# Mixer attention ordered by query block, with the last block's selection rounds between its units, and score matmuls of two heads issued in turn

## The chip, the cores and the metric

The kernel runs on one core of a Trainium2 chip. The metric is device time in microseconds (us) of one execution, the median of the runs shown. Profiled executions are single ones; their own time stands beside their span.

## The reference

A sequence of 512 tokens of width 1024 goes through two blocks, all in float32. The first block has a pooling layer and an attention layer with 16 heads of 64 in three groups of dilations 1, 4 and 16, each followed by a gated feed-forward layer. The second block has two layers, each with a feed-forward layer, a mixer and another feed-forward layer. The mixer is what the change is mostly about. In short:

```
p = h @ w_in                       # u, va, q, k, v, iq, ik, iw
a_out = gelu(u) * (tril(w_s) @ gelu(va) + b_s)            # gating, chunks of 128
score[t, s] = sum_h iw[t, h] * relu(iq[t, h] . ik[s])     # 4 index heads, s <= t
keep = the 128 largest of score[t, :]
b_out = softmax(q k^T / 8 over keep) v                    # 8 heads of 64
y = concat(a_out, b_out) @ w_out
```

## The kernel before, in words

Every float32 product is made of three matmuls on a high and a low part: high x high, high x low, low x high (`mm3`, L1701). Weights arrive in slabs of 128 x 1024; ScalarE rounds a slab to its high part (`split_hi`, L604), VectorE (`split_lo`, L1024) or, for slabs 10 to 22 of a mixer projection, GpSimd (`project_lo`, L564) subtracts to get the low part. Two split slabs exist at a time. Engines are ordered by hand: each has its own program, and semaphores count steps.

**Projection (`project`, L1859 on TensorE, L1276 on VectorE, L738 on ScalarE).** 23 slabs, of which the last two are left to the mixer. In slots 6 to 8 TensorE makes the index scores of query blocks 1 to 3 (`index_scores`, L1889): for each block four heads, head by head, each with its three matmuls; heads alternate between partitions 0 to 63 and 64 to 127, since one head has 64 of the 128 rows. ScalarE takes the relu, VectorE adds them up with their weights into `score`. Then 16 selection rounds follow (`topk_round`, L1397; `ROUNDS`, L1341, says how many after which slab). A round finds the eight largest of each row (MAX8, L1400) and overwrites them (MATCH_REPLACE8, L1406), for blocks 1, 2 and 3 of 256, 384 and 512 columns. At the end the overwritten places become the mask (L1393). Block 0 keeps everything causal.

**Mixer (`mix`, L1950 on TensorE, L816 on ScalarE, L1427 on VectorE).** 32 units u, a head and a query block each; head u // 4 and block u % 4, so that the width n goes 128, 256, 384, 512 over and over. For a unit, TensorE makes the scores (L1956) in one of three PSUM banks, three units ahead; VectorE adds the mask and takes the row minimum of the negated scores (`mask_scores`, L1432); ScalarE takes the exponential and its sum (L841); TensorE transposes the n / 128 blocks (L2035); ScalarE writes their high part (`probs_hi`, L822), VectorE the low part (`probs_lo`, L1442). After the four units of a head TensorE multiplies with the values (`values`, L1965), 12 matmuls over 512, 384, 256 and 128 columns, and ScalarE copies the output (`o_out`, L831). TensorE fills its time: in units 0 to 7 the rest of the projection (`last_u`, L1988), in units 16 to 31 the gated half of the output projection (`first_part`, L2002), six matmuls of 512 columns a unit (`FILL`, L449). In units 9 to 12 the gating matmuls stand (`sgu`, L1978), VectorE follows with two operations (`sgu`, L1411) and a low part (`sgu_lo`, L1423). ScalarE's gelus of two tiles (L853) stand in unit 8, with a change of its table to gelu and back. At the end the reciprocal sums are transposed (L2048), split and spread over the heads' rows (L2057, L2058), multiplied in (L1494), and the rest of the output projection (`out_rest`, L2060) begins.

**First attention (`dilated_attention`, L2079).** 22 steps: the six heads of dilation 1 have two steps of two blocks, the other ten heads one step of four blocks of 128. Score banks are three (`SCORE_BANKS`, L404), and scores run three steps ahead, one step after each step's transposes. After the last step of a head its values follow.

## Time and profile before

| | us |
|---|---|
| runs (three) | 3250.24, 3252.34, 3247.52; median 3250.24 |
| profiled execution, its own time | 3245.89 |
| its span | 3244.2 |
| mean granted clock of TensorE | 0.973 of full |
| TensorE busy | 3110.7 |
| VectorE busy | 1751.6 |
| ScalarE busy | 1193.7 |
| first attention, first to last transposes | 668.4 to 729.0 |
| first mixer, first fill to the rest of the output projection | 1701.4 to 1806.3 |
| second mixer, first fill to the last transposes | 2733.2 to 2828.8 |

A busy share is the time in which an engine executes something; matmuls are pipelined, so a busy TensorE can still be at a fraction of its rate, and the start times of neighbouring matmuls tell more than their durations. A wait is put down to the instruction that released it last. The stretches used below: 1653.9 to 1700.0 is the end of the first mixer's projection; 1701.4 to 1723.3 has units 0 to 7 (from the first fill to the transposes of unit 8); 1723.3 to 1750.6 units 8 to 15; 1750.6 to 1797.0 the rest up to the transposes of unit 31; 1797.0 to 1806.3 the tail. 668.4 to 700.1 has the twelve steps of dilation 1 in the first attention, 700.1 to 729.0 the other ten.

### The profile page before, as it was taken

What the parts mean: (1) busy time and instruction counts of PE and PEld (TensorE: products, weight loads), DVE (VectorE), ACT (ScalarE), POOL (GpSimd) and SP (SyncE); (2) the same over time, 40 slices, a digit from 0 to 9 for tenths busy, and PEclk for the clock granted to TensorE, in tenths of its full rate; (3) what the DMA queues carried; (4) which work ended last, traced back from release to release, by engine and by line L of the source; (5) the groups of instructions that cost most, each with busy time, mean ns of one, the idle gap of its engine ahead of it and who ended that gap; (6) DMA issues with size and microseconds to landing.
All of it is one profiled execution on the core that took longest, in us unless ns stands there. A gap on an engine that the chain in (4) does not pass through costs nothing.

```text
span 3244.2 us, 38749 instructions
## 1 busy us (share of the span) xinstructions
PE 3110.7 (96%) x14007; PEld 2546.1 (78%) x14007; DVE 1751.6 (54%) x2784; ACT 1193.7 (37%) x1687; POOL 124.9 (4%) x117
## 2 busy tenths in 40 slices
PE   7899999999999999999999999999999998899998
PEld 5788888877888878888776788887888876678887
DVE  5577535655785366634684666324332576553323
ACT  3332323463233244432334443324442334444422
POOL 0000000000000000000030000000000012000000
PEclk8999999988999999999899999999999999899999
DMA  3355333203554335533220355322333322023332
GB/s 116 122 183 186 106 97 95 89 20 96 183 187 136 97 117 187 174 95 98 70 83 22 115 189 187 98 94 85 96 97 97 96 72 65 27 82 95 96 103 78
DMA packets 262904, 351.28 MB, mean 108 GB/s; under 512 B 16664, under 2 KB 208536, under 8 KB 262808
## 3 DMA queue, kind: packets, MB, share of 16 engines
q1 hardware_dynamic: 240768, 270.57, 26.9%
q0 software_dynamic: 21360, 79.01, 7.5%
q8 instruction: 60, 0.98, 0.1%
q10 hardware_dynamic: 680, 0.43, 0.0%
q14 instruction: 36, 0.29, 0.0%
HBM read 348.75 MB, written 2.10 MB: 108 GB/s over the span
## 4 chain that ended last, share of the span: by engine, by line
PE 84%; DVE 9%; ACT 4%; issue 2%; DMA 0%; POOL 0%; SPq 0%; DVEq 0%; ACTq 0%
PE bank L1703 28%; PE bank L1704 27%; PE bank L1705 27%; ACT w_hi L613 1%; DVE a_score L1406 1%; DVE a_m L1400 1%; DVE w_lo L1028 1%; DVE rot L1309 1%; DVE sumsq L1041 1%; PE bank L2035 1%; DVE work L1081 1%; DVE turned L1308 0%; DVE h_lo L1087 0%; PE bank L1744 0%; ACT probs L900 0%
## 5 line engine op out<-in xcount | busy, mean ns | idle before, releaser
L1028 DVE TENSOR_TENSOR w_lo<-raw,w_hi 128x1024 fp32r<-128x1024 f32 x482 | 589.7, 1224 | 1195.4 <-ACT w_hi L613 1194.8
L1703 PE MATMUL bank<-h_hi,w_hi 128*128 128x512 f32 x2864 | 1137.8, 397 | 28.3 <-POOL w_lo L571 11.7
L1705 PE MATMUL bank<-h_hi,w_lo 128*128 128x512 f32 x2864 | 1125.1, 393 | 0.0
L1704 PE MATMUL bank<-h_lo,w_hi 128*128 128x512 f32 x2864 | 1124.1, 393 | 0.0
L613 ACT ACTIVATE w_hi<-raw 128x1024 fp32r<-128x1024 f32 x508 | 537.6, 1059 | 1364.4 <-PE bank L1705 1359.9
L1703 PEld LDWEIGHTS bank<-h_hi,w_hi 128*128 128x128 f32 x2864 | 543.6, 190 | 158.1 <-issue 41.1
L1705 PEld LDWEIGHTS bank<-h_hi,w_lo 128*128 128x128 f32 x2864 | 543.1, 190 | 115.6
L1704 PEld LDWEIGHTS bank<-h_lo,w_hi 128*128 128x128 f32 x2864 | 544.2, 190 | 109.8
L1703 PE MATMUL bank<-act_hi,w_hi 128*128 (+1 forms) x1120 | 435.9, 389 | 1.0 <-DVE w_lo L1028 1.0
L1705 PE MATMUL bank<-act_hi,w_lo 128*128 (+1 forms) x1120 | 435.7, 389 | 0.0
L1704 PE MATMUL bank<-act_lo,w_hi 128*128 (+1 forms) x1120 | 435.7, 389 | 0.0
L1703 PEld LDWEIGHTS bank<-act_hi,w_hi 128*128 128x128 f32 x1120 | 210.3, 188 | 45.2 <-issue 1.4
L1705 PEld LDWEIGHTS bank<-act_hi,w_lo 128*128 128x128 f32 x1120 | 210.3, 188 | 43.5
L1704 PEld LDWEIGHTS bank<-act_lo,w_hi 128*128 128x128 f32 x1120 | 210.3, 188 | 43.5
L1109 DVE SCALAR_TENSOR_TENSOR ada_acc<-ada_w,cact,ada_acc 128x512 f32<-128x512 f32 x252 | 189.2, 751 | 7.7
L698 ACT ACTIVATE act_hi<-work 128x512 f32 (+1 forms) x132 | 82.1, 633 | 161.2 <-DVE work L1148 89.5
L533 POOL DMA_DIRECT2D ada_w<-in_ada_w_dram x72 | 54.3, 755 | 1414.4 <-DVE ada_acc L1109 988.5
L1151 DVE TENSOR_TENSOR act_lo<-work,act_hi 128x512 f32 (+1 forms) x132 | 87.0, 692 | 20.6 <-ACT act_hi L698 20.4
L1438 DVE CUSTOM_DVE_ANT_0 bank<-bank,a_masks 128x128 f32<-128x128 f32 (+1 forms) x64 | 31.9, 499 | 94.8 <-PE bank L1705 94.7
L571 POOL TENSOR_TENSOR w_lo<-raw,w_hi 128x1024 fp32r<-128x1024 f32 x26 | 61.8, 2387 | 254.4 <-ACT w_hi L613 254.4
L613 ACT ACT_TABLE_LOAD x45 | 57.7, 1283 | 7.8 <-issue 7.0
L630 ACT ACTIVATE sq<-xT 128x512 f32<-128x512 f32 x70 | 43.8, 627 | 36.3 <-DVE xT L1092 33.1
(288 smaller groups left out, 2368.3 us busy)
## 6 DMA issues: line engine op xcount, KB each, us to landing
raw<-in_ffn_w_in_dram SPq DMA_DIRECT2D x176, 512.0 KB, 3.5
ada_w<-in_ada_w_dram POOLq DMA_DIRECT2D x72, 1024.0 KB, 5.6
raw<-in_ffn_w_out_dram SPq DMA_DIRECT2D x88, 512.0 KB, 3.7
raw<-in_ffn_w_gate_dram SPq DMA_DIRECT2D x44, 512.0 KB, 3.8
raw<-in_ffn_w_up_dram SPq DMA_DIRECT2D x44, 512.0 KB, 3.8
raw<-in_ffn_w_down_dram SPq DMA_DIRECT2D x44, 512.0 KB, 3.7
raw<-in_mix_w_in_dram SPq DMA_DIRECT2D x44, 512.0 KB, 3.6
raw<-in_attn_w_qkv_dram SPq DMA_DIRECT2D x24, 512.0 KB, 3.6
```

The costliest lines, as they stand in the source:

```text
L533: pool.dma_start(ada_w[:, half], w[:, 4 * half:4 * half + 4, bass.ds(i * 512 + (f % 2) * N_MOD * 512, 512)])\
L571: nc.gpsimd.tensor_tensor(w_lo[:, n % SPL, :], raw[:, n % RAW, :], w_hi[:, n % SPL, :].bitcast(F32), ALU.subtract).then_inc(s_lo, 1)
L613: nc.scalar.activation(w_hi[:, nb % SPL, :], raw[:, nb % RAW, :], ACT.Copy).then_inc(s_hi, 1)
L630: nc.scalar.activation(part, xT[:, k, :], ACT.Square, scale=size).then_inc(s_sq, 1)
L698: nc.scalar.activation(act_hi[:, bass.ds(i * 2 + c, 1), :], work[:, 2 + c:3 + c, :], ACT.Copy).then_inc(s_ahi, 1)
L1028: V.tensor_tensor(w_lo[:, nb % SPL, :], raw[:, nb % RAW, :], w_hi[:, nb % SPL, :].bitcast(F32), ALU.subtract).then_inc(s_lo, 1)
L1041: V.tensor_tensor(total, total, part, ALU.add).then_inc(s_sum, 1)
L1109: ins = V.scalar_tensor_tensor(out=ada_acc[:], in0=w, scalar=cact[:, k:k + 1], in1=ada_acc[:], op0=ALU.mult, op1=ALU.add)
L1151: V.tensor_tensor(act_lo[:, bass.ds(i * 2 + c, 1), :], work[:, 2 + c:3 + c, :], act_hi[:, bass.ds(i * 2 + c, 1), :].bitcast(F32), ALU.subt ...
L1703: T.matmul(dst, wh, mh, start=first, stop=False)
L1704: T.matmul(dst, wh, ml, start=False, stop=False)
L1705: return T.matmul(dst, wl, mh, start=False, stop=last)
```

## The change

- **Order of units.** Unit u is head u % 8 of query block u // 8, so the widths are 128 for units 0 to 7, 256 for 8 to 15, 384, then 512. Probabilities have a ring of three, and values are made per unit (two units behind its transposes) in matmuls of 128 columns, 3 (b + 1) of them for block b. `o_out` copies four heads of a block by two instructions. 240 value matmuls take the place of 96.
- **Selection.** `topk_round` in the projection has blocks 1 and 2 only. VectorE makes the 16 rounds of block 3 in units 0 to 15 of the mixer, one in each: MAX8 ahead of the mask of unit u + 2, MATCH_REPLACE8 behind it and ahead of the low part of unit u. The mask of block 3 is made at unit 16.
- **Scores of two heads in turn.** The scores of a pair of heads (rows 0 to 63 and 64 to 127, two PSUM banks) are issued as one group, the same term of either head in turn, at every second unit and two units ahead; so too the index scores (which now wait for both relus before), and in the first attention, where the steps of dilation 1 are reordered to (h, 0), (h + 1, 0), (h, 3), (h + 1, 3), four banks are used and a pair of steps is issued at every odd step.
- **Moved.** Output fills stand in units 14 to 29, gating matmuls in 8 to 11, VectorE's gating in 8 to 11 with low parts in 10 to 13, additions to x from unit 16, slab splits of the output projection from 18 and 19 on. The first scores wait for the gelus of two tiles. The reciprocal sums come at unit 31 ahead of its low part; their transposes and ScalarE's copy of them come ahead of the last values and output copies. GpSimd's two waits for all values count units instead of heads.

The diff, cut to its core (indentation shortened):

```diff
-SCORE_BANKS = (0, 1, 6)
+STEP_BANKS = (0, 1, 6, 7)
...
-for h in range(HEAD_GROUPS[0][1]):
-    A0.append((h, 0, [(4 * h, 0, 0, 0, P, 0), (4 * h + 1, P, 0, P, 2 * P, P)]))
-    A0.append((h, 3, [(4 * h + 2, 2 * P, P, 0, 2 * P, P), (4 * h + 3, 3 * P, 2 * P, 2 * P, 2 * P, P)]))
+for pair_at in range(0, HEAD_GROUPS[0][1], 2):
+    for h in (pair_at, pair_at + 1):
+        A0.append((h, 0, [(4 * h, 0, 0, 0, P, 0), (4 * h + 1, P, 0, P, 2 * P, P)]))
+    for h in (pair_at, pair_at + 1):
+        A0.append((h, 3, [(4 * h + 2, 2 * P, P, 0, 2 * P, P), (4 * h + 3, 3 * P, 2 * P, 2 * P, 2 * P, P)]))
...
-FILL = {u: ("u", 2 * u) for u in range(8)} | {u: ("out", 2 * (u - 16)) for u in range(16, 32)}
+FILL = {u: ("u", 2 * u) for u in range(8)} | {u: ("out", 2 * (u - 14)) for u in range(14, 30)}
...
-            h, b = u // 4, u % 4
+            n = (u // 8 + 1) * P
             act.wait_ge(s_tr, u0 + u + 1)
-            if b == 0 and h >= 2:
-                act.wait_ge(s_pv, h0 + h - 1)
-            dst = b_["PTh"][:, h % 2, :].rearrange("p (n q) -> p n q", q=P)[:, b:b + 3 * b + 1:3, :]
-            nc.scalar.activation(dst, bank[2 + u % 2][:, 0:(b + 1) * P].rearrange("p (n q) -> p n q", q=P), ACT.Copy)\
-                .then_inc(s_pth, 1)
-        def o_out(h):
-            act.wait_ge(s_pv, h0 + h + 1)
-            rows = slice(HD * (h % 2), HD * (h % 2) + HD)
-            nc.scalar.activation(b_["oT"][rows, h // 2, :], bank[4][0:HD, :], ACT.Copy).then_inc(s_o, 1)
+            if u >= 3:
+                act.wait_ge(s_pv, t["p0"] + u - 2)
+            nc.scalar.activation(b_["PTh"][:, u % 3, 0:n], bank[2 + u % 2][:, 0:n], ACT.Copy).then_inc(s_pth, 1)
+        def o_out(g):
+            b, j = g // 2, 2 * (g % 2)
+            act.wait_ge(s_pv, t["p0"] + 4 * g + 4)
+            for x in range(2):
+                ins = nc.scalar.activation(b_["oT"][HD * x:HD * x + HD, j:j + 2, b * P:(b + 1) * P],
+                                           bank[4][0:HD, 2 * x * P:2 * x * P + 2 * P].rearrange("p (n q) -> p n q", q=P),
+                                           ACT.Copy)
+            ins.then_inc(s_o, 1)
...
-                        topk_round(bufs, (1, 2, 3))
+                        topk_round(bufs, (1, 2))
...
-        for u in range(3):
+        for u in range(2):
             mask_scores(u)
         for u in range(nu):
-            if u + 3 < nu:
-                mask_scores(u + 3)
+            if u < 16:
+                dve.wait_ge(s_dve, steps[0])
+                largest()
+            if u == 16:
+                dve.wait_ge(s_dve, steps[0])
+                keep_taken(bufs, 3)
+            if u + 2 < nu:
+                mask_scores(u + 2)
+            if u < 16:
+                take_largest()
+            if u == nu - 1:
+                dve.wait_ge(s_exp, u0 + nu)
+                V.reciprocal(bufs["fine"][:, 5, :, 0:nh], bufs["den"][:, 0:nu].rearrange("p (b h) -> p b h", b=NB))\
+                    .then_inc(s_on, 1)
...
+            y, b, j = 12 * (m - 1) + x0, x0 // 4 + 1, x0 % 4 // 2
+            if x0 == 0:
+                pe.wait_ge(s_post, PO0[m] + 3)
+                pe.wait_ge(s_wi, m)
+            else:
+                pe.wait_ge(s_relu, y)
+            q, k = slice(b * P, (b + 1) * P), slice(0, (b + 1) * P)
+            for n, (a, c) in enumerate((("iqTh", "ikTh"), ("iqTh", "ikTl"), ("iqTl", "ikTh"))):
+                for x in (0, 1):
+                    r = slice(HD * x, HD * x + HD)
+                    ins = T.matmul(bank[6 + x][:, k], bufs[a][r, j, q], bufs[c][r, 0, k], start=n == 0, stop=n == 2)
+                    if n == 2:
+                        ins.then_inc(s_idxmm, 1)
...
+            b, j = u // 8, u % 8 // 2
+            if u >= 2:
+                pe.wait_ge(s_exp, u0 + u - 1)
             q, k = slice(b * P, (b + 1) * P), slice(0, (b + 1) * P)
-            mm3(bank[MIX_BANKS[u % 3]][:, k], bufs["qTh"][r, h // 2, q], bufs["qTl"][r, h // 2, q],
-                bufs["kTh"][r, h // 2, k], bufs["kTl"][r, h // 2, k], True, True).then_inc(s_scmm, 1)
-        def values(h):
-            c = h // 2
-            pe.wait_ge(s_pt, u0 + 4 * h + 4)
-            if h:
-                pe.wait_ge(s_o, t["h0"] + h)
-            for k in range(NB):
-                v = slice(c * P + HD * (h % 2), c * P + HD * (h % 2) + HD)
-                pt = slice(4 * k * P, 4 * k * P + (NB - k) * P)
-                ins = mm3(bank[4][0:HD, k * P:S], bufs["vNh"][:, k, v], bufs["vNl"][:, k, v],
-                          bufs["PTh"][:, h % 2, pt], bufs[f"PTl{h % 2}"][:, pt], k == 0, k == NB - 1)
+            for n, (a, c) in enumerate((("qTh", "kTh"), ("qTh", "kTl"), ("qTl", "kTh"))):
+                for x in range(2):
+                    r = slice(HD * x, HD * x + HD)
+                    ins = T.matmul(bank[MIX_BANKS[(u + x) % 3]][:, k], bufs[a][r, j, q], bufs[c][r, j, k],
+                                   start=n == 0, stop=n == 2)
+                    if n == 2:
+                        ins.then_inc(s_scmm, 1)
+        def values(u):
+            b, h = u // 8, u % 8
+            pe.wait_ge(s_pt, u0 + u + 1)
+            if u % 4 == 0 and u:
+                pe.wait_ge(s_o, t["h0"] + u // 4)
+            at = (h % 4 // 2 + 2 * (h % 2)) * P
+            for k in range(b + 1):
+                v = slice(h * HD, h * HD + HD)
+                pt = slice(k * P, (k + 1) * P)
+                ins = mm3(bank[4][0:HD, at:at + P], bufs["vNh"][:, k, v], bufs["vNl"][:, k, v],
+                          bufs["PTh"][:, u % 3, pt], bufs["PTl"][:, u % 3, pt], k == 0, k == b)
...
+        pe.wait_ge(s_actT, AT0[f"out{m}"] - 2)
         scores(0)
-        pe.wait_ge(s_actT, AT0[f"out{m}"] - 2)
-        scores(1)
-        scores(2)
         for u in range(nu):
             if u in FILL:
                 what, step = FILL[u]
             pe.wait_ge(s_exp, u0 + u + 1)
             if u >= 2:
                 pe.wait_ge(s_pt, u0 + u - 1)
-            for k in range(u % 4 + 1):
+            for k in range(u // 8 + 1):
                 ins = T.transpose(bank[2 + u % 2][:, k * P:(k + 1) * P], bufs["P"][:, u % 2, k * P:(k + 1) * P], ident)
             ins.then_inc(s_tr, 1)
-            if u + 3 < nu:
-                scores(u + 3)
-            if 9 <= u < 13:
-                sgu(u - 9)
-            if u % 4 == 1 and u >= 5:
-                values(u // 4 - 1)
-        values(nh - 1)
-        pe.wait_ge(s_hlo, H0[f"attn{m}"] + 4)
+            if u % 2 == 0 and u + 2 < nu:
+                scores(u + 2)
+            if 8 <= u < 12:
+                sgu(u - 8)
+            if u >= 2:
+                values(u - 2)
+        values(nu - 2)
         pe.wait_ge(s_on, OT0[m] + 1)
         for b in range(NB):
             ins = T.transpose(bank[6][0:nh, b * P:(b + 1) * P], bufs["fine"][:, 5, b, 0:nh], ident)
         ins.then_inc(s_otr, 1)
+        values(nu - 1)
...
-            if s >= 3:
+            if s >= 4:
                 pe.wait_ge(s_exp, s - 2)
-            h = A0[s][0]
-            r = slice(HD * (h % 2), HD * (h % 2) + HD)
-            for _, q, k, off, n, _ in A0[s][2]:
-                ins = mm3(bank[SCORE_BANKS[s % 3]][:, off:off + n], bufs["qTh"][r, h // 2, q:q + P],
-                          bufs["qTl"][r, h // 2, q:q + P], bufs["kTh"][r, h // 2, k:k + n], bufs["kTl"][r, h // 2, k:k + n],
-                          True, True)
-            ins.then_inc(s_scmm, 1)
+            j, blocks = A0[s][0] // 2, A0[s][2]
+            for i, (_, q, k, off, n, _) in enumerate(blocks):
+                for t, (a, c) in enumerate((("qTh", "kTh"), ("qTh", "kTl"), ("qTl", "kTh"))):
+                    for x in (0, 1):
+                        r = slice(HD * x, HD * x + HD)
+                        ins = T.matmul(bank[STEP_BANKS[(s + x) % 4]][:, off:off + n], bufs[a][r, j, q:q + P],
+                                       bufs[c][r, j, k:k + n], start=t == 0, stop=t == 2)
+                        if i == len(blocks) - 1 and t == 2:
+                            ins.then_inc(s_scmm, 1)
...
-        for s in range(3):
-            scores(s)
+        scores(0)
+        scores(2)
         for s in range(n_steps):
             pe.wait_ge(s_exp, s + 1)
             if s >= 2:
             for k in range(width(A0[s]) // P):
                 ins = T.transpose(bank[2 + s % 2][:, k * P:(k + 1) * P], bufs["P"][:, s % 2, k * P:(k + 1) * P], ident)
             ins.then_inc(s_tr, 1)
-            if s + 3 < n_steps:
+            if s % 2 and s + 3 < n_steps:
```

## Rows read from the trace of the kernel before

**Rows 1.** The page: span, and busy time of each engine.

```profile
span 3244.2 us, 38749 instructions
...
PE 3110.7 (96%) x14007; PEld 2546.1 (78%) x14007; DVE 1751.6 (54%) x2784; ACT 1193.7 (37%) x1687; POOL 124.9 (4%) x117
```

**Rows 2.** By stretch: length; PE, PEld, DVE, ACT, POOL busy; granted clock; DMA share; GB/s.

```profile
1653.90:1700.00 46.10, 38.46 (x171) 31.07 (x171) 37.66 (x108) 15.19 (x23) 17.29 (x8) 0.96 0.27 80
1701.40:1723.30 21.90, 21.90 (x105) 15.86 (x105) 7.89 (x26) 9.95 (x30) 0.00 (x0) 1.00 0.16 49
1723.30:1750.60 27.30, 20.24 (x95) 14.83 (x95) 15.12 (x33) 14.17 (x32) 0.00 (x0) 0.75 0.06 20
1750.60:1797.00 46.40, 46.07 (x228) 33.68 (x229) 23.21 (x59) 20.75 (x56) 0.00 (x0) 1.00 0.11 33
1797.00:1806.30 9.30, 5.89 (x30) 3.44 (x27) 5.11 (x9) 3.00 (x5) 1.55 (x2) 0.93 0.36 119
668.40:700.10 31.70, 31.28 (x194) 26.70 (x194) 17.75 (x72) 21.24 (x73) 0.00 (x0) 0.79 0.00 1
700.10:729.00 28.90, 25.45 (x231) 22.57 (x231) 17.09 (x78) 26.16 (x93) 0.00 (x0) 0.94 0.01 1
```

**Rows 3.** Waits, 1560 to 1700 us (first mixer projection): total, times, longest.

```profile
ACT L812 <- DVE a_vNl L1290: 9.7, 1, 9.7
...
PE bank L1703 <- POOL w_lo L571: 5.9, 3, 2.8
```

**Rows 4.** Order of time (start, us): matmuls on PE behind the third stall.

```profile
1685.82 0.63 PE L1703 MATMUL bank<-h_hi,w_hi 128*128 128x512 f32 x1
1686.24 0.63 PE L1704 MATMUL bank<-h_lo,w_hi 128*128 128x512 f32 x1
```

**Rows 5.** VectorE by form, 1600 to 1807 us: busy, mean ns, idle before.

```profile
L1406 DVE MATCH_REPLACE8 a_score<-a_m,a_score 128x512 f32<-128x512 f32 x16 | 10.8, 676 | 0.0
L1400 DVE MAX8 a_m<-a_score 128x8 f32<-128x512 f32 x16 | 10.8, 676 | 0.0
...
L1028 DVE TENSOR_TENSOR w_lo<-raw,w_hi 128x1024 fp32r<-128x1024 f32 x7 | 8.5, 1217 | 2.2 <-ACT w_hi L613 2.2
...
L1406 DVE MATCH_VALUE_LOAD a_score<-a_m,a_score 128x8 f32 x48 | 3.8, 78 | 0.0
L1438 DVE CUSTOM_DVE_ANT_0 bank<-bank,a_masks 128x256 f32<-128x256 f32 x8 | 3.5, 433 | 16.3 <-PE bank L1705 16.3
...
L1425 DVE TENSOR_TENSOR h_lo<-work,h_hi 128x512 fp32r<-128x512 f32 x4 | 2.7, 681 | 0.0
...
L1447 DVE TENSOR_TENSOR a_probsT_lo<-bank,probsT_hi 128x256 fp32r<-128x256 f32 x4 | 1.7, 422 | 1.9 <-ACT probsT_hi L828 1.9
```

**Rows 6.** Order of time: index scores of two heads, opposite row halves.

```profile
1602.82 0.40 PE L1704 MATMUL bank<-a_ikTl,a_iqTh 64*128 64x512 f32 x2
1603.05 0.40 PE L1705 MATMUL bank<-a_ikTh,a_iqTl 64*128 64x512 f32 x2
```

**Rows 7.** Order of time: mixer scores of one head, then a fill.

```profile
1713.52 0.39 PE L1704 MATMUL bank<-a_kTl,a_qTh 64*128 64x512 f32 x1
...
1713.75 0.39 PE L1705 MATMUL bank<-a_kTh,a_qTl 64*128 64x512 f32 x1
...
1714.07 0.50 PE L1703 MATMUL bank<-h_hi,w_hi 128*128 128x512 f32 x1
```

**Rows 8.** Order of time: first and last of 12 value matmuls, 128 columns.

```profile
716.01 0.27 PE L1703 MATMUL bank<-a_probsT_hi,h_hi 128*64 128x128 f32 x1
...
716.71 0.22 PE L1705 MATMUL bank<-a_probsT_hi,h_lo 128*64 128x128 f32 x1
```

**Rows 9.** Order of time: the gelu pause of the mixer.

```profile
1728.71 0.29 DVE L1447 TENSOR_TENSOR probsT_lo<-bank,probsT_hi 128x128 fp32r<-128x128 f32 x1 [3.40 <-ACT probsT_hi L828]
```

**Rows 10.** Order of time: last transposes, start of the coefficient spreading.

```profile
1796.86 0.60 PE L2035 MATMUL bank<-squares,probs 128*128 128x128 f32 x4
...
1802.87 0.47 PE L2057 MATMUL bank<-a_cTh,sel 8*128 8x512 f32 x1 [1.61 <-issue]
```

99 lines of the change are left out of this document (43 added, 56 removed).

## The prediction

> **What bounds the kernel now.** The page comes first: TensorE is busy 96% of the span, VectorE 54%, ScalarE 37% [rows 1]. A share over the whole span says little on three stages that the change touches, so I cut them into stretches next [rows 2]. In the mixer of the first mixer layer, units 0 to 7 take 21.9 us and TensorE is busy all of it at full clock: TensorE is the bound. Units 8 to 15 take 27.3 us, TensorE busy 20.2 of them at a granted clock of 0.75 (between the levels of 1.2 and 2.4 GHz): here a chain over ScalarE and VectorE sets the pace. Units 16 to 31 take 46.4 us with TensorE busy 46.1: TensorE again. The tail to the rest of the output projection is 9.3 us with 5.9 busy. The second mixer layer has the same stretches to 0.1 us, so every term below counts twice. The first attention has a half where TensorE is busy 31.3 of 31.7 us at clock 0.79, and a half where ScalarE is busy 26.2 of 28.9 us.
>
> The waits of the projection show what the page hides: TensorE waits 5.9 us in three stalls for slabs split by GpSimd, and ScalarE, which feeds GpSimd, sits 9.7 us behind a value tile of VectorE [rows 3]. VectorE is busy 37.7 us of that 46.1 us stretch [rows 2], with selection rounds. So VectorE, not the weights, ends those stalls. Behind the third stall matmuls start 0.42 us apart [rows 4] where 0.23 us is usual [rows 7]; the stretch's clock of 0.96 means 8% of 46.1 us at the lower level, half of which is lost, 1.8 us.
>
> **Projection.** Sixteen rounds on the last block leave it, each a MAX8 and a MATCH_REPLACE8 on 512 columns with a value load: 0.676 + 0.676 + 0.078 = 1.43 us [rows 5], together 22.9 us of VectorE. That is four times the stalls. What is late next is the ordinary slab chain, which keeps up where VectorE isn't in it. Ceiling 5.9 + 1.8 = 7.7 us, floor 3 (one stall, the longest being 2.8, goes); I take 6.5, near the ceiling, since the relief is so much larger than the stall.
>
> **Index scores.** The program issues three matmuls of one head, then three of the next in the other row half, but they start in twos, 0.23 us per two [rows 6]. They run side by side already, so interleaving them by hand costs and brings nothing; the wait for both older relus may add some 0.5 us, inside the bounds. The Trainium skill (TensorE: Matmul & The Clock Gate, Part 3) says that matmuls are strictly ordered by program in start and end. By that rule the two heads could not have overlapped before and the twelve head-blocks (about 6 us a layer at 384 columns each) would now halve, the total falling 6 us more; the measurement decides against it.
>
> **Mixer, units 0 to 7.** A unit is now a head of query block 0. Its TensorE work falls: score pairs side by side, half as many changes between full-row and half-row matmuls; 48 fill matmuls at 0.23 us stay (11.0), the rest falls from 10.9 to about 5. But VectorE gets a round per unit: 1.43 + mask 0.43 + low part 0.42 = 2.28 [rows 5] (the forms of 256 columns, a bound from above for 128), eight times 18.2, and one slab split of 1.2. TensorE 16, VectorE at most 19.4: I take 18.5, so -3.4; between -4.5 and 0. The round sits in VectorE's order ahead of the low part of the same unit, for which the transposes of the unit after next wait; up to there TensorE may run ahead.
>
> **Units 8 to 15.** The gelu pause of ScalarE stays: its first low part comes at 1728.71, 5.4 us into the stretch [rows 2, 9]. From there VectorE has, for units 8 to 13, five rounds with mask (1.86 each, 9.3), six low parts (2.5), four gating pairs and four of their low parts (12 x 0.68 = 8.2), a slab split (1.2): 21.2 us. Then a new wait: the output fills start at unit 14 instead of 16, and the first needs the last gating low part of unit 13. TensorE then owes three fills (18 x 0.23 = 4.1), transposes (four, 0.11 each [rows 10]), a score pair (0.7) and twelve value matmuls at 0.064 (0.70 / 11) [rows 8]: 6.0 us before the transposes of unit 16. Sum 5.4 + 21.2 + 6.0 = 32.6 against 27.3: +5.3. Bounds: 0 if instructions overlap as they do in rounds of three blocks and the fills slip under VectorE, +10 if TensorE is at the lower clock there. I take the sum.
>
> **Units 16 to 31.** Now: 96 fill matmuls at 0.23 (22.1), scores 15360 columns at 0.45 ns, from 0.23 us for 512 (6.9), 40 transposes (4.4), values 15360 columns (6.9): 40.3. The other 6.1 us are 32 changes of row mode, 0.19 each; 0.09 of one is seen directly, 0.32 instead of 0.23 [rows 7]. Afterwards: 13 fills remain behind the first transposes (78 x 0.23 = 17.9); 19200 score columns in twos (4.3); 52 transposes (5.7); 144 value matmuls at 0.064 (9.2); 14 changes (2.7). That is 39.8, and about 1.2 at the end, where units 30 and 31 have no fill to cover their exponentials: 41.0, -5.4. VectorE is busy 23.2 us of this stretch now [rows 2] and gets one mask of 0.4 us more, so TensorE's work hides it; without that cover the mask and low part of a unit would stand on the path. Bounds -7 and -1 (the latter without overlap of pairs).
>
> **Tail.** The last values shrink from 3840 columns (1.7) to 12 short matmuls (0.8), and the coefficients are turned and split ahead of them, which takes the 1.6 us of issue wait [rows 10] and their own transposes; two output copies come behind the values instead of one. -2.7, between -3.5 and -1.
>
> **First attention.** The first half loses half of 16128 score columns (7.3 us, more at clock 0.79) and half its mode changes, but ScalarE's 21.2 us and its chain are near: -3. The second half has ScalarE at 26.2 of 28.9 us: -1. Bounds -8 (ScalarE's own time) and +2 (longer stretches at the lower clock, since two steps' scores now stand ahead of each values).
>
> **Sum.** Mixer -3.4 + 5.3 - 5.4 - 2.7 = -6.2; with -6.5 a layer gives -12.7; twice -25.4; first attention -4: -29.4 us. The profiled execution took 3245.9 us (span 3244.2 and 1.7 around it), so 3216.5; it lies 4.3 below the median of the three runs, so 3221 for a median.
>
> **Rivals.** (A) The sum above, 3212 to 3233. (B) VectorE's rounds are absorbed: units 8 to 15 keep 27.3 us and the first attention gains two more: 3221 - 10.6 - 2 = 3208. For it: back-to-back VectorE records overlap. Against: gating and rounds fall together. (C) The change doesn't do what it says: float pairs of 64 rows in the mixer don't run side by side. Third stretch +4.3, first +1, twice, and 4 in the first attention: 3236. The index pairs speak against it [rows 6]. (D) Slower: the rounds bound units 0 to 15. There VectorE's 7.9 + 15.1 busy us [rows 2] and 22.9 make 45.9 of a present 49.2, and each low part waits behind a match. The forecast exposes 1.9 us of the 22.9 a layer; gains elsewhere are 6.5 + 5.4 + 2.7 + 2 = 16.6. Above that the kernel is slower; wholly exposed, (22.9 - 16.6) x 2 = +12.6: 3263. Against it: TensorE's queue runs ahead by up to two units. (E) The clock: should the thinner TensorE work of units 8 to 15 and short matmuls keep it at 1.2 GHz for 23 of the 41 us of the third stretch, 11.5 us a layer go back, 3244, and no change can be told. Against it: that stretch ran at 1.00 behind one at 0.75.
>
> **Chances.** A 0.60, B 0.16, C 0.12, E 0.05, D 0.07. A measurement here tells about 0.2%, 6.5 us, from no change; A, B and C are faster by more, E the same, D slower. Range 3205 to 3241: A whole, most of B, and C.
>
> **What would show it.** Projection: no wait of ScalarE for a value tile of 9 us, TensorE's wait for GpSimd near 0. Units 0 to 7 about 18.5 us, VectorE over 90% busy; 8 to 15 about 33 us with a wait ahead of the fill of unit 14; from the transposes of unit 16 to those of 31 about 41 us, TensorE without waits; mixer scores of two heads starting in twos 0.23 us apart at 512 columns. The forecast is wrong if the 5.9 us stay, or if VectorE ends TensorE's waits throughout.

## The result, and the profile after

The changed kernel takes 3209.9 us (median of four runs, 3209.0 to 3216.6) against 3248.9 for the kernel before (four runs, 3246.9 to 3252.3): a ratio of 0.988, 95% interval 0.986 to 0.990. It is faster by 39 us. The forecast was 3221 us in a range of 3205 to 3241, so the direction and the range were right, and the size was 10 us short: 3209.9 lies below the 3212 to 3233 us that the prediction gave its own sum (rival A), and 2 us from the 3208 of rival B.

The profiled execution took 3216.56 us, 29.3 less than the profiled one of before (3245.89). That is the -29.4 of the sum almost to the digit, and largely by accident, as the next table shows: this execution lies 6.6 us above the median of its own kernel. A second profile of the same kernel was therefore taken beside the experiments (`after_again`, own time 3208.30). The table has starts of transposes, read from the order of time of each trace; differences between neighbouring rows give the stretches.

| us from the start | before | after | after_again |
|---|---|---|---|
| first attention, first transposes | 668.39 | 669.16 | 666.75 |
| first attention, last transposes | 728.74 | 727.40 | 720.65 |
| first mixer, unit 0 | 1702.90 | 1693.97 | 1687.53 |
| unit 8 | 1723.30 | 1709.81 | 1703.33 |
| unit 16 | 1753.68 | 1744.20 | 1737.72 |
| unit 31 | 1796.86 | 1784.70 | 1778.17 |
| second mixer, unit 0 | 2733.79 | 2710.84 | 2704.25 |
| unit 8 | 2754.25 | 2726.81 | 2718.80 |
| unit 16 | 2784.55 | 2759.80 | 2752.47 |
| unit 31 | 2827.68 | 2800.30 | 2792.98 |
| own time | 3245.89 | 3216.56 | 3208.30 |

From before to after_again, in that order: first attention 60.4 to 53.9 (-6.4); from there to unit 0, which holds the first projection, -7.3; units 0 to 7 20.4 to 15.8 (-4.6) and in the second layer 20.5 to 14.6 (-5.9); units 8 to 15 30.4 to 34.4 (+4.0) and 30.3 to 33.7 (+3.4); units 16 to 31 43.2 to 40.5 (-2.7) and -2.6; from unit 31 to the unit 0 of the second layer (tail, feed-forward layers, second projection) 936.9 to 926.1 (-10.8); the rest -2.9, and the part before the first attention -1.6. The two profiles of the changed kernel differ mostly in the first attention (58.2 against 53.9).

The page of the changed kernel, answering [rows 1]. TensorE has 29 us less to do, VectorE as much as before: the change took nothing from it, it only moved it.

```profile
span 3214.9 us, 39389 instructions
...
PE 3081.5 (96%) x14295; PEld 2536.7 (79%) x14295; DVE 1752.3 (55%) x2784; ACT 1199.2 (37%) x1703; POOL 125.3 (4%) x117
```

By stretch, with the columns of [rows 2]: the end of the first projection, units 0 to 7, units 8 to 15, units 16 to 31, the tail, and the two halves of the first attention.

```profile
1646.00:1691.50 45.50, 42.92 (x210) 35.83 (x209) 26.20 (x82) 19.72 (x28) 19.16 (x8) 0.98 0.28 81
1692.00:1709.80 17.80, 17.80 (x98) 13.51 (x97) 13.43 (x44) 8.56 (x29) 0.00 (x0) 0.87 0.12 40
1709.80:1744.20 34.40, 22.58 (x136) 18.41 (x135) 26.67 (x68) 15.93 (x40) 0.00 (x0) 0.70 0.08 25
1744.20:1784.70 40.50, 40.02 (x318) 32.21 (x316) 25.07 (x53) 22.87 (x54) 0.00 (x0) 1.00 0.13 40
1784.70:1792.00 7.30, 6.20 (x56) 4.43 (x55) 4.97 (x9) 3.58 (x7) 1.54 (x2) 1.00 0.17 39
669.20:699.40 30.20, 26.53 (x198) 22.48 (x199) 19.19 (x78) 20.81 (x72) 0.00 (x0) 0.73 0.00 1
699.40:727.40 28.00, 21.79 (x219) 18.78 (x217) 15.24 (x69) 26.20 (x93) 0.00 (x0) 0.87 0.01 1
```

In the first line TensorE is now busy 42.9 of 45.5 us where it was 38.5 of 46.1. In the third, no engine is busy throughout: TensorE 22.6, VectorE 26.7, ScalarE 15.9 of 34.4 us. Such a stretch is a chain, and the experiments are mostly about which chain. For the third and fourth line a warning on the cut: in [rows 2] the stretch of units 16 to 31 began at the transposes of unit 15 (1750.51) and so held the fill of unit 16 and the 3.2 us up to the transposes of that unit, while the fourth line here begins at the transposes of unit 16. The table above cuts both kernels at unit 16.

The waits of the projection, 1550 to 1690 us: what answers to [rows 3] is this.

```profile
ACT st_v L811 <- DVE a_vNl L1292: 2.4, 1, 2.4
...
ACT L811 <- DVE a_vNl L1292: 0.4, 1, 0.4
```

ScalarE's 9.7 us behind a value tile are gone, and TensorE's 5.9 us behind GpSimd's low parts no longer appear. VectorE even has time to spare there. In the waits of 1590 to 1694 us it idles 17.1 us at one go, up to the mixer's first scores, where the longest such wait in the kernel before is 8.1 us:

```profile
DVE bank L1444 <- PE bank L1992: 17.1, 1, 17.1
```

One thing came in that no term of the prediction has. The first scores now wait for the gelus of two tiles. In the kernel before, TensorE had two waits there, with the scores of unit 0 between them (first fence); in the changed kernel it stands still for 2.58 us at one go (second fence):

```profile
1699.35 0.33 PE L1703 MATMUL bank<-a_kTh,a_qTh 64*128 64x128 f32 x1 [1.51 <-ACT a_vaN L780]
...
1700.33 0.38 PE L1703 MATMUL bank<-a_kTh,a_qTh 64*128 64x256 f32 x1 [0.43 <-ACT a_uT L802]
```

```profile
1690.41 0.48 PE L1992 MATMUL bank<-a_kTh,a_qTh 64*128 64x128 f32 x2 [2.58 <-ACT a_uT L801]
```

From the first fill to the transposes of unit 8 the granted clock is 1.00 in the profile of before and 0.85 in the changed kernel (1691.25 to 1709.81). That the single wait is the reason is not shown: a variant of the kernel before, with the same two waits, falls to the lower clock right behind them too (section on pairs).

The order of time in units 8 to 15 shows the gelu pause as in [rows 9], and the new wait at unit 14. The columns are start, duration, engine.

```profile
1715.63 0.42 DVE L1451 TENSOR_TENSOR probsT_lo<-bank,probsT_hi 128x256 fp32r<-128x256 f32 x1 [2.70 <-ACT probsT_hi L826]
...
1734.33 0.68 DVE L1429 TENSOR_TENSOR h_lo<-work,h_hi 128x512 fp32r<-128x512 f32 x1
...
1735.11 0.77 PE L1728 MATMUL bank<-h_hi,w_hi 128*128 128x512 f32 x1 [2.66 <-issue]
1735.67 0.63 PE L1729 MATMUL bank<-h_lo,w_hi 128*128 128x512 f32 x1
...
1739.84 0.57 DVE L1444 CUSTOM_DVE_ANT_0 bank<-bank,a_masks 128x384 f32<-128x384 f32 x1 [4.23 <-PE bank L1992]
```

The last gating low part begins at 1734.33 and the first output fill follows at 1735.11, behind 2.66 us of idle TensorE; its matmuls stand 0.43 us apart, at the lower clock. The transposes of unit 14 stand behind that fill in TensorE's order, VectorE then waits 4.23 us for the scores behind them. Units 16 to 31 have no wait of size, and scores of two heads start together, 0.23 us per two at 512 columns:

```profile
1772.71 0.39 PE L1992 MATMUL bank<-a_kTl,a_qTh 64*128 64x512 f32 x2
1772.94 0.39 PE L1992 MATMUL bank<-a_kTh,a_qTl 64*128 64x512 f32 x2
```

### The profile page after: what moved, and what is told of

Read it like the earlier page. It is cut to its first block, busy times and chain, and to the rows that moved or that the text cites. A ratio compares the mean times of both kernels' runs of the same rounds, so it can differ in the third digit from the quotient of the medians.

```text
span 3214.9 us, 39389 instructions
## 1 busy us (share of the span) xinstructions
PE 3081.5 (96%) x14295; PEld 2536.7 (79%) x14295; DVE 1752.3 (55%) x2784; ACT 1199.2 (37%) x1703; POOL 125.3 (4%) x117
## 3 DMA queue, kind: packets, MB, share of 16 engines
q8 instruction: 62, 1.02, 0.1%
## 4 chain that ended last, share of the span: by engine, by line
PE 88%; DVE 6%; ACT 3%; issue 2%; DMA 0%; SPq 0%; DVEq 0%; ACTq 0%
PE bank L1728 28%; PE bank L1730 28%; PE bank L1729 28%; DVE w_lo L1030 1%; ACT w_hi L612 1%; DVE sumsq L1043 1%; PE bank L1992 1%; DVE work L1083 1%; PE bank L2066 0%; DVE h_lo L1089 0%; ACT probs L902 0%; PE bank L2124 0%; PE bank L1769 0%; DMA raw<-in_pool_w_in_dram 0%; DVE xT L1094 0%
## 5 line engine op out<-in xcount | busy, mean ns | idle before, releaser
L1153 DVE TENSOR_TENSOR act_lo<-work,act_hi 128x512 f32 (+1 forms) x132 | 87.0, 692 | 20.6 <-ACT act_hi L697 20.4
L1444 DVE CUSTOM_DVE_ANT_0 bank<-bank,a_masks 128x128 f32<-128x128 f32 (+3 forms) x64 | 31.3, 491 | 70.8 <-PE bank L1992 70.8
```

Of the source, the lines that this page charges most:

```text
L1153: V.tensor_tensor(act_lo[:, bass.ds(i * 2 + c, 1), :], work[:, 2 + c:3 + c, :], act_hi[:, bass.ds(i * 2 + c, 1), :].bitcast(F32), ALU.subt ...
```

## The experiments

Times are medians of four or more runs, ratios are to the kernel before on the same chip; "against 3209.6" means the changed kernel, measured again as a base. The experiments ran in four groups on four chips, on which the kernel before has medians of 3248.7 to 3250.4 us, so a difference of 1 or 2 us between groups settles nothing by itself. Small differences are read from the stretches of the traces.

> The changed kernel itself, as the base for the runs beside it on the same chip. Both theories expect 0.9877 of the kernel before, about 3210 us, and in the first mixer 15.8 us for units 0 to 7, 34.4 for units 8 to 15 and 40.5 for units 16 to 31.

Measured: 3209.59 us, ratio 0.9882 (0.9868 to 0.9896).

### The rounds back in the projection

All 16 rounds of block 3, and the mask made from them, go back to where the kernel before has them.

```diff
-                                topk_round(bufs, (1, 2))
+                                topk_round(bufs, (1, 2, 3))
...
-                    if u < 16:
-                        dve.wait_ge(s_dve, steps[0])
-                        largest()
...
-                    if u < 16:
-                        take_largest()
```

> All 16 rounds of block 3 go back into the projection, the rest of the change stays. Theory 1 (VectorE's rounds stall the projection and, moved, stretch units 8 to 15): TensorE's waits for GpSimd's slabs come back, 6 to 8 us a layer; units 8 to 15 lose the six rounds of units 8 to 13, 8.6 us, and go from 34.4 to about 26; units 0 to 7 keep 15.8 us, since TensorE is the bound there. Net -1 us a layer, 3208 us. Theory 2 (the rounds hide in units 0 to 15 at no cost, and the stage is long for its cold clock and the gelu pause): units 8 to 15 stay at 34, the projection costs 7 a layer again, 3224 us.

Measured: 3223.22 us, 0.9927 (0.9914 to 0.9940), 13.6 more than the changed kernel. The waits of 1550 to 1700 us have all of [rows 3] back:

```profile
ACT L811 <- DVE a_vNl L1292: 9.7, 1, 9.7
ACT st_v L811 <- DVE a_vNl L1292: 9.5, 1, 9.5
...
PE bank L1720 <- POOL w_lo L570: 5.9, 3, 2.8
```

From the first attention's last transposes to unit 0, and from unit 31 to the next unit 0, the kernel is 7.9 and 7.1 us longer than after_again: that is the worth of the projection step. From unit 8 to unit 16 it takes 32.5 us (1712.51 to 1745.03) instead of 34.4, in the second layer 32.4 instead of 33.7. So the 11.4 us of VectorE's work that left the stretch (eight rounds at 1.43) were worth 1.9 and 1.3 us. Units 0 to 7 are 1.2 us longer in the first layer and the same in the second. Together 7.9 + 7.1 + 1.2 - 1.9 - 1.3 = 13.0 of the 13.6. Theory 2 gave the time, and it is right that the rounds are not what makes units 8 to 15 long; but it named only the gelu pause and the clock, and something else holds the stretch at 32 us without a single round.

### The ring

In units 8 to 12 VectorE's gating of a tile, ScalarE's high part of it ("the copy" below), the next exponential, the next probabilities' high part, VectorE's low part and its gating stand one behind the other. Two edits separate this ring from VectorE's own load: eight rounds moved into its 17.1 us of idle time, and ScalarE's copy one unit later.

```diff
                     for b in (1, 2):
                         keep_taken(bufs, b)
+                    for _ in range(8):
+                        topk_round(bufs, (3,))
...
-                    if u < 16:
+                    if u < 8:
```

```diff
-                    if 9 <= u < 13:
-                        g = u - 9
+                    if 10 <= u < 14:
+                        g = u - 10
```

> Eight of the 16 rounds of block 3 run in the 17.1 us that VectorE idles at the end of a projection; units 0 to 7 keep one each, units 8 to 15 have none. Changed kernel: 3209.6 us, units 8 to 15 34.4 us, four of them 4.08 us apart. Theory R (a ring: ScalarE's gating copy sits between an exponential and the next and waits for VectorE's gating of the same unit, so a unit cannot be shorter than copy 0.63 + exponential 0.65 + high part 0.37 + low part 0.41 + gating low part 0.68 + gating 1.3 = 4.0 us, rounds or not): units stay 4.0 us apart, the stretch falls by 1 to 2 us, 3206 us. Theory V (VectorE's own work sets those units, 1.27 us of rounds in each): units 2.8 us apart, the stretch falls by 7 to 8, 3195 us.

> ScalarE's copy of a gated tile comes one unit later in its order (units 10 to 13 instead of 9 to 12); rounds stay in units 0 to 15. Theory R: the ring is opened, but VectorE with its round is busy 3.85 of the 4.08 us, so units become at most 0.2 us shorter: 3207 to 3210 us. Theory V: the same, since VectorE is the bound either way. A third, that the ring alone sets the units and records overlap further: 3200 us.

> Both edits: eight rounds early and the copy a unit later. Theory R: each of the two was a bound of its own, so only together they free the stage: VectorE 4.08 less 1.27 = 2.8 us a unit, five units, and the fills after unit 13 start sooner; the stretch of units 8 to 15 falls by 6 to 7 us, twice: 3196 us. Theory V: no more than eight rounds early alone gives. Rival (the lower clock and the gelu pause set the stage): no more than 2 us a layer, 3206 us.

Measured: rounds early alone 3206.58 us, 0.9857 (0.9833 to 0.9880); copy later alone 3210.62, 0.9872 (0.9848 to 0.9896); both 3200.86, 0.9841 (0.9817 to 0.9865). Against 3209.6 that is -3.0, +1.0 (not to be told from nothing), and -8.7 together, where -2.0 would be the sum of the two. The traces are clearer: of units 8 to 15 the three leave 32.0, 33.7 and 27.9 us out of 34.4 in the first layer, and 32.0, 34.4 and 27.3 out of 33.7 in the second.

The order of time of the first one (rounds gone from these units) shows the ring, one turn of it:

```profile
1719.84 0.63 ACT L859 ACTIVATE h_hi<-work 128x512 fp32r<-128x512 f32 x1 [2.64 <-DVE work L1427]
...
1720.38 0.46 ACT L843 ACTIVATE probs<-bank,a_nmx 128x256 f32<-128x256 f32 x1
...
1720.82 0.37 ACT L826 ACTIVATE probsT_hi<-bank 128x256 fp32r<-128x256 f32 x1
...
1721.23 0.42 DVE L1453 TENSOR_TENSOR probsT_lo<-bank,probsT_hi 128x256 fp32r<-128x256 f32 x1 [1.02 <-ACT probsT_hi L826]
1721.57 0.68 DVE L1431 TENSOR_TENSOR h_lo<-work,h_hi 128x512 fp32r<-128x512 f32 x1
...
1722.39 0.69 DVE L1425 TENSOR_TENSOR work<-bank,a_bbc 128x512 f32<-128x512 f32 x1
...
1723.11 0.69 DVE L1427 TENSOR_TENSOR work<-work,a_uT 128x512 f32<-128x512 f32 x1
...
1723.84 0.63 ACT L859 ACTIVATE h_hi<-work 128x512 fp32r<-128x512 f32 x1 [2.64 <-DVE work L1427]
```

From copy to copy it is 4.00 us, ScalarE waits 2.64 of them for VectorE and VectorE 1.02 for ScalarE: both engines wait in every turn, so neither is the bound. With the rounds in, VectorE has 1.27 us more a turn and fills that 1.02 up: the turn is 4.08 in the changed kernel. That is why the rounds cost nearly nothing there. With the copy late alone, units 9 to 12 came 2.3 to 3.3 us apart, and then VectorE, which with its rounds was busy without a gap from 1709.8 to 1729.8 us, was late with the last gating low part: TensorE waited 6.4 us for it, and unit 14 came 9.9 us behind unit 13 (1722.10 to 1731.96). Only both edits free the units: 2.1 to 2.5 us from one to the next in the first layer. What was left then is the wait at the fill, 3.5 us in the waits of that kernel from 1705 to 1733 us:

```profile
PE bank L1730 <- DVE h_lo L1431: 3.5, 1, 3.5
```

The same edit in the kernel before asks whether the ring is older than the change.

```diff
-                    if 10 <= u < 14:
-                        g = u - 10
+                    if 11 <= u < 15:
+                        g = u - 11
```

> The kernel before with one edit: ScalarE's copy of a gated tile a unit later (units 11 to 14). Theory R says the ring was there before the change: its units 9 to 12 stand 4.0 us apart on average with four heads of all widths, and VectorE alone needs about 3 us for one, so the stretch falls by 2 to 4 us a layer, 3243 us. Rival (the ring is a product of the new order): 3249 us.

Measured: 3242.09 us, 0.9975 (0.9962 to 0.9989), -7.1 against 3249.2. Units 8 to 15 fall from 30.4 to 26.8 us. The ring was there before the change, and opening it is worth 3.6 and 3.2 us in the two layers. Units 0 to 7, which the edit doesn't touch, are 2.4 and 0.6 us longer in this one profile; the section on pairs comes back to it.

### The output fills

```diff
-        FILL = ... | {u: ("out", 2 * (u - 14)) for u in range(14, 30)}
+        FILL = ... | {u: ("out", 2 * (u - 16)) for u in range(16, 32)}
```

with the additions to x from unit 18 and the slab splits of ScalarE and VectorE from 20 and 21 on, as in the kernel before.

> The changed kernel (3209.6 us, stretch of units 8 to 15 34.4 us, of 16 to 31 40.5) with the output fills, their additions to x and slab splits back at units 16 to 31. Theory 1 (the fill of unit 14 waits for the last gating low part and holds the transposes of units 14 and 15 behind it): the first stretch falls by the two fills and the wait, 34.4 to about 28, the second gains two fills at full clock, 2.8 us, 40.5 to 43.5, and the tail keeps a cover for units 30 and 31: 2 to 3 us a layer less, 3205 us. Theory 2 (the fills only change place): 3 to 4 us go from one stretch to the other, 3209 us. Theory 3 (TensorE without them stays at its lower clock longer into unit 16 and on): slower, 3213 us.

Measured: 3202.22 us, 0.9851 (0.9821 to 0.9881), -7.4: more than any theory gave. Units 8 to 15, then 16 to 31:

```profile
1704.18:1731.58 27.40, 17.82 (x123) 14.56 (x122) 24.30 (x62) 15.15 (x38) 0.00 (x0) 0.75 0.10 31
1731.58:1774.36 42.78, 42.78 (x329) 34.56 (x330) 27.90 (x62) 24.27 (x56) 0.00 (x0) 1.00 0.10 30
```

The first loses 7.0 us (5.8 in the second layer) and the second gains 2.3 (2.2). At unit 14 TensorE's fill cost 2.7 us of idle time and six matmuls at 0.43 us before the transposes of that unit could be made, while the next units waited. Moved behind unit 15, the twelve matmuls of the two fills run at 0.23 us in a stretch where TensorE is the bound, and cost about their own time there (2.8 us). The order of units, rounds and pairs is untouched: moving the fills forward, taken alone, made the changed kernel 7.4 us slower.

### Pairs

First the order within a pair, at all three places where scores are paired:

```diff
-                    for n, (a, c) in enumerate((("qTh", "kTh"), ("qTh", "kTl"), ("qTl", "kTh"))):
-                        for x in range(2):
+                    for x in range(2):
+                        for n, (a, c) in enumerate((("qTh", "kTh"), ("qTh", "kTl"), ("qTl", "kTh"))):
```

> All paired scores (index, mixer, first attention) keep their places and waits, but within a pair the three matmuls of one head are issued, then the three of the other. Theory 1 (triples of opposite row halves run side by side in this order too, as the index scores of the kernel before did): no difference, 3210 us, starts still in twos. Theory 2 (strict order; only neighbours in the program can overlap, so A A A B B B overlaps once in six): score columns count fully. Mixer stretch 16 to 31 about +3.6 us (half of 7.2 less one overlap in three), all scores of a layer with the index scores about +8, first attention +3: 3229 us.

Measured: 3209.88 us, 0.9883 (0.9869 to 0.9898), nothing. The trace of this kernel, whose program has three matmuls of one head and then three of the other, shows starts in twos all the same:

```profile
1767.28 0.50 PE L1992 MATMUL bank<-a_kTh,a_qTh 64*128 64x512 f32 x2
1767.61 0.40 PE L1992 MATMUL bank<-a_kTl,a_qTh 64*128 64x512 f32 x2
1767.85 0.40 PE L1992 MATMUL bank<-a_kTh,a_qTl 64*128 64x512 f32 x2
```

Then the pairs themselves, in the mixer only:

```diff
                 def scores(u):
-                    b, j = u // 8, u % 8 // 2
-                    if u >= 2:
-                        pe.wait_ge(s_exp, u0 + u - 1)
+                    b, j, x = u // 8, u % 8 // 2, u % 2
+                    if u >= 3:
+                        pe.wait_ge(s_exp, u0 + u - 2)
...
+                    mm3(bank[MIX_BANKS[u % 3]][:, k], bufs["qTh"][r, j, q], bufs["qTl"][r, j, q],
+                        bufs["kTh"][r, j, k], bufs["kTl"][r, j, k], True, True).then_inc(s_scmm, 1)
...
                 scores(0)
+                scores(1)
+                scores(2)
...
-                    if u % 2 == 0 and u + 2 < nu:
-                        scores(u + 2)
+                    if u + 3 < nu:
+                        scores(u + 3)
```

So scores also run three units ahead again instead of two, and wait for another exponential.

> The mixer's scores one head at a time at every unit, three units ahead as in the kernel before; order by block, rounds and the rest as in the changed kernel. Theory 1 (pairs halve their columns' time, and with them go half the changes of row mode): in units 16 to 31, 9600 more columns at 0.45 ns are 4.3 us and 8 to 16 more changes at 0.19 are 1.5 to 3, together 6 to 7 us more, with 1 to 2 in units 0 to 7, twice: 3225 us. Theory 2 (the stretch gained through order and tail, not pairs): at most 2 us a layer, 3213 us.

Measured: 3239.85 us, 0.9959 (0.9942 to 0.9976), +30.3 against an expected 15. Units 16 to 31 behave as worked out: 46.4 us in both layers against 40.5, +5.9. The surprise is in units 0 to 7. Stretches of this kernel (columns: length, TensorE busy, granted clock, DMA share, GB/s), units 0 to 7 of the first and second layer, then units 16 to 31:

```profile
1689.35:1710.56 21.21, 21.21 (x93) 0.79 0.09 27
2716.61:2739.41 22.80, 22.80 (x94) 0.72 0.07 23
1744.28:1790.66 46.38, 45.89 (x314) 1.00 0.11 35
```

and the same of the changed kernel (after_again):

```profile
1687.53:1703.33 15.80, 15.80 (x93) 0.91 0.06 17
2704.25:2718.80 14.55, 14.55 (x93) 1.00 0.06 19
1737.72:1778.17 40.45, 39.96 (x318) 1.00 0.13 41
```

TensorE is busy all the time in all four stretches of units 0 to 7, but without pairs its clock stays at 1.2 GHz far longer. Around the 2.6 us in which it waits for the gelus it falls to that level in both kernels. In the first layer of the changed kernel it is back about 6 us after the wait, without pairs it is still there 12 us on:

```profile
1684.00:1690.00 6.00, 6.00 (x22) 0.50 0.27 87
1690.00:1698.00 8.00, 8.00 (x50) 0.98 0.02 4
```

```profile
1686.00:1698.00 12.00, 12.00 (x35) 0.50 0.14 46
1700.00:1708.00 8.00, 8.00 (x45) 1.00 0.03 4
```

With two levels of which one is half the other, a stretch at a mean clock c loses 1 - c of its length. In units 0 to 7 of the first layer that is 0.21 x 21.2 = 4.5 us against 0.09 x 15.8 = 1.4, so 3.1 of the extra 5.4 us are the clock and 2.3 are columns and changes of row mode. In the second layer it is 0.28 x 22.8 = 6.4 against 0, of 8.2 extra, and 1.8 are left. So by this reckoning the clock in units 0 to 7 is 9.5 of the 30 us. Units 16 to 31 are 11.8 (5.9 twice, all at full clock) and units 8 to 15 are 1.8 (-0.7 and +2.5); the last 3 us lie outside the units, where nothing was changed.

The clock differs from execution to execution, so two stretches alone would be thin. Eleven profiles have pairs in the mixer, with two layers each. Read in steps of 0.5 us, in 13 of these 22 places the clock is at the lower level for 6.8 us in all, in 8 for 3.4 us, and in one (second layer, with the rounds back) not at all. Without pairs it is 13.7 and 17.1 us, outside all of them, and over the whole span the mean granted clock is 0.967 in the median of the ten runs against 0.971 in that of the changed kernel's eight. Yet it is not the missing pairs alone. The kernel before has none either, and its profile stays at full clock in both layers, while the variant with the copy one unit later has 6.8 and 3.4 us at the lower level. There units 0 to 7 have scores of 128 to 512 columns, here of 128 only.

No experiment takes the order of the units back by itself. The pieces that were taken back singly (rounds 13.6, first attention 4.4, pairs 30.3, fills -7.4) come to 40.9 us where the whole change is 39, but since they depend on each other this is no division of the gain, and what the order alone is worth stays open.

### The first attention

```diff
-        STEP_BANKS = (0, 1, 6, 7)
+        STEP_BANKS = (0, 1, 6)
...
-                scores(0)
-                scores(2)
+                for s in range(3):
+                    scores(s)
```

and the order of steps and the `scores` of the kernel before.

> The first attention as in the kernel before (order of steps, three banks, one step's scores at a time), the rest of the change stays. Theory 1: the part is worth what the two profiles show, 2 us of first attention, 3212 us. Theory 2: it is worth the predicted 4 us and one profile fell badly, 3214 us. Theory 3: it is worth nothing or costs time, because it puts TensorE at its lower clock: 3208 to 3210 us.

Measured: 3213.97 us, 0.9913 (0.9891 to 0.9934), 4.4 more, with runs that scatter from 3212.3 to 3231.4; the two intervals touch, so the runs alone settle its sign but weakly. The stretches of the traces are firmer. From the first to the last transposes the old arrangement takes 60.4, 58.3 and 60.3 us in its three profiles (before, this one, and the last of the ring's experiments), the new one 53.9 to 54.1 in ten of its eleven and 58.2 in one: the profile that stands under the result. The part from 695 us on, of this kernel and of after_again:

```profile
695.00:727.49 32.49, 28.31 (x268) 25.14 (x267) 19.88 (x92) 29.13 (x106) 0.00 (x0) 1.00 0.01 2
```

```profile
695.00:720.65 25.65, 19.09 (x212) 15.76 (x210) 15.52 (x69) 25.45 (x92) 0.00 (x0) 0.94 0.01 2
```

ScalarE is busy 25.45 of the last 25.65 us: with pairs this part stands on ScalarE's own work, and nothing more is to be had from TensorE there.

### A version that beats both

Rounds early, copy late and fills from unit 16 together:

> Eight rounds early, ScalarE's copy a unit later, and the fills from unit 16: a version meant to beat both kernels. Without the last edit it took 3200.9 us, its units 8 to 15 27.9 us, with a wait of TensorE for the last gating low part of 3.5 us. Theory 1: that wait goes, 1 to 3 us a layer: 3197 us. Theory 2: the fills only change place: 3201 us. Theory 3 (clock): 3204 us.

Measured: 3193.00 us, 0.9818 (0.9793 to 0.9843); units 8 to 15 take 23.4 us. Then ScalarE's split of the second output slab from unit 8 to 14 and VectorE's from 9 to 15:

```diff
+                    if u == 14:
+                        split_hi(out + 1)
                     if u == 8:
-                        split_hi(out + 1)
...
-                    if u == 9:
+                    if u == 15:
                         split_lo(out + 1)
```

> The best version so far (3193.0 us) with the split of the second output slab taken out of the stretch's critical chains: ScalarE's high part from unit 8, where it stands 1.05 us ahead of the gelus, to unit 14, VectorE's low part (1.22 us) from unit 9 to unit 15. Theory R (a chain over ScalarE and VectorE sets units 8 to 13): 1 us at the gelus and up to 1.2 us in VectorE's order go, 1 to 2 us a layer, 3190 us. Rival (these are covered, or the slab is then late for unit 20): no change or slower, 3193 to 3196 us.

Measured: 3189.17 us, 0.9814 (0.9801 to 0.9827), 20.4 us below the changed kernel. Its two stretches:

```profile
1704.13:1726.52 22.39, 16.40 (x124) 13.67 (x123) 16.97 (x44) 15.68 (x40) 0.00 (x0) 0.82 0.04 14
1726.52:1770.08 43.56, 43.56 (x329) 35.10 (x328) 25.73 (x55) 23.75 (x54) 0.00 (x0) 0.97 0.13 41
```

Units 8 to 15 are down from 34.4 to 22.4 us, 1.0 less than without the last edit. But units 16 to 31 are 0.9 us longer than without it, at a clock of 0.97, and in the second layer it is -1.1 and +1.0. In the traces the last edit thus brings nothing in the two stretches together, and the ratios of the two versions, 0.9818 and 0.9814, can't be told apart: that moving the split gained anything is not shown. What beats both kernels are the three edits before it.

## Why the prediction was right, and where it was short

**Projection (-6.5 taken, ceiling 7.7): right, and the ceiling was reached.** The experiment with the rounds back gives 7.9 and 7.1 us, cut at unit 0. The marks named for it appeared: no long wait of ScalarE for a value tile, none of TensorE for GpSimd.

**Index scores (0): right.** Interleaving by hand changes nothing, at any of the three places. The wait for both relus cost what was allowed: ahead of one pair TensorE waits 2.4 us for a relu, 1.9 before.

**Units 0 to 7 (-3.4): the size right by luck, the bound wrong.** From the first fill (1691.25) to the transposes of unit 8 it is 18.6 us, 18.5 forecast. But VectorE, said to be over 90% busy and to set the 18.5, is busy 13.4 of 17.8 us; the forms of 128 columns are cheaper than the bound from above. TensorE is the bound, at a mean clock of 0.85. By the reckoning of the section on pairs that loses 0.15 x 18.6 = 2.8 us, and the 15.8 left are the 16 that the prediction had put down for TensorE alone. The lower clock, for which no term stood, happened to put back what VectorE was wrongly charged with. Where TensorE is not at that clock, in the second layer of after_again from unit 0 to 8, it takes 14.6 us instead of 15.8.

**Units 8 to 15 (+5.3 to 32.6 us): 34.4, the step whose mechanism was wrong.** The sum took the gelu pause (5.4), VectorE's chain to the last gating low part (21.2) and TensorE's work behind it (6.0). Measured are 5.8 (to 1715.63), 19.4 (to the end of that low part, 1735.0) and 9.2 (to 1744.20, at a mean clock of 0.66, by which 3.1 us of it are lost). The increase itself is on two cuts, since 32.6 us reach to the transposes of unit 16 and the 27.3 they are set against only to those of unit 15. On one cut the forecast is +2.2 (30.4 to 32.6) here and -2.2 (43.2 to 41.0) in units 16 to 31, against +4.0 and -2.7 measured; in the sum the slip cancels. The first two terms nearly came out, and still VectorE was not the bound: take eight rounds away and the stretch is 2.4 us shorter (1.6 in the second layer), not 11. It was one of two chains of nearly one length, 4.0 and 4.1 us a unit. The prediction never looked for the other, though the waits of the kernel before (1728 to 1748 us) had it:

```profile
ACT h_hi L857 <- DVE work L1421: 7.4, 3, 2.9
```

In the same way the new wait at unit 14 was priced at its own work, while what it cost was that all later units stood behind it: 7.0 and 5.8 us in the two layers against 2.3 and 2.2 given back. Rival B, where the rounds are absorbed, was nearer to the mechanism: they are. It lost its point because the fills moved at the same time.

**Units 16 to 31 (-5.4): right.** With the prediction's own cut 46.4 to 40.5, -5.9. Pairs carry it: without them the stretch takes 46.4 us, 3.2 more than the 43.2 of the kernel before on the same cut. With the fills back it is 42.8 us, so 2.3 us of the gain only came over from the stretch ahead.

**Tail (-2.7): -2.1**, from the transposes of unit 31 to the rest of the output projection 9.3 to 7.2 us.

**First attention (-4): -6.4 in most executions, -2.1 in the profiled one**, 4.4 by the medians. Both halves were mis-sized by 1.2 us: in after_again the twelve steps of dilation 1 take 27.4 us instead of 31.6 (-4.2, -3 taken) and the other ten 26.5 instead of 28.7 (-2.2, -1 taken), and what is left of the second is ScalarE's own time.

**Sum.** It fell 8 to 10 us short. after_again lies 37.6 us below the profile of before, 8.2 more than the sum. By its own steps, with units 0 to 7 cut at the transposes of unit 0, the shortfall is: projections 3.0 (-7.3, and -10.8 less 2.1 of tail, against -6.5 twice), first attention 2.4, units 0 to 7 3.7 (-10.5 against -6.8); to the other side units 8 to 31 2.2 (+2.0 against -0.2) and the tails 1.2. The last 2.4 lie ahead of the first attention (1.6) and behind the second tail (0.8), where the change touches nothing, and belong to the scatter of executions. Cut at the first fill, as the prediction has it, units 0 to 7 are -3.4 and -4.7, so 1.3 of the 3.7 are theirs and the rest is the projections'. That the profiled execution agreed with the sum to 0.1 us was chance: its first attention ended 6.7 us later than that of after_again.

**The rival of a slower kernel** (VectorE bounds units 0 to 15) was refuted by the same experiment as the forecast's own term, and rival C, that pairs don't overlap, by the twos in the trace. That the clock might take back a gain (rival E) was put in units 16 to 31, where it stayed at 1.00. It was at work in units 0 to 7: 0.85 where the kernel before has 1.00, 2.8 us of the first layer.

## What to carry to other kernels

Where no engine is busy throughout a stretch, look for a ring through two engines before adding up one engine's work: an instruction that sits between two links of another chain in its engine's order closes one, and two bounds of nearly one length show nothing until both are lifted. A fill belongs where the engine is the bound, not where it first becomes possible: put ahead of a link of a chain, it costs everything behind it. And compare a sum with more than one profiled execution before believing that its terms are right.

## What the runs showed of the hardware

**Matmuls of opposite row halves don't keep the program's order.** Besides the twos above, the trace of the kernel before has a pair of index scores whose second head was released late. The program has all three of the first head, then those of the second:

```profile
1608.64 0.39 PE L1704 MATMUL bank<-a_ikTl,a_iqTh 64*128 64x512 f32 x1
1608.80 0.49 PE L1703 MATMUL bank<-a_ikTh,a_iqTh 64*128 64x512 f32 x1
1608.88 0.39 PE L1705 MATMUL bank<-a_ikTh,a_iqTl 64*128 64x512 f32 x1
```

The first matmul of the second head (L1703, 1608.80) starts ahead of the last one of the first (L1705, 1608.88). The Trainium skill (TensorE: Matmul & The Clock Gate, Part 3) states strict order in start and end; these rows and the experiment on the order within a pair differ from it, and the measurement decides.

**In the order by query block the clock stayed at its lower level for 13.7 and 17.1 us when half-row matmuls came one at a time, and for 6.8 us or less in 22 places where they came in pairs**, TensorE being busy without a gap behind the same wait of 2.6 us (rows in the section on pairs). In the old order, without pairs, it was 6.8 us or less as well, so the pairs are not the whole of it, and what in the work makes the difference was not tried. In the experiment without pairs the clock is 9.5 of the 30 us.
